# Two narrow fp32 matmuls in place of eighteen in the matmul stream of a two-block transformer kernel

## The reference, cut to what matters

```python
hn = _rmsnorm(x, norm_mix[0]);  x = x + _moba(hn, w_qkv, w_o)          # attention, 16 heads
x = x + _conv_ffn(_rmsnorm(x, norm_ffn[0]), w_up, conv_w, conv_b, w_down)
x = _rmsnorm(x, norm_final)
# second block, with shift, scale and gate vectors from c @ w_mod + b_mod
h = modulate(rms_norm(x, g_ffn1), sh1, sc1)
x = x + 0.5 * (1 + ga1) * swiglu(h, w1_gate, w1_up, w1_down)
h = modulate(rms_norm(x, g_mix), sh2, sc2)
x = x + (1 + ga2) * hybrid_mixer(h, w_in, b_f, g_q, g_k, w_o)          # attention, 8 + 8 heads
h = modulate(rms_norm(x, g_ffn2), sh3, sc3)
x = x + 0.5 * (1 + ga3) * swiglu(h, w2_gate, w2_up, w2_down)
```

## Time and profile before

| | us |
|---|---|
| median of 3 timed executions | 839.67 |
| lowest and highest of them | 838.92, 843.66 |
| the profiled execution, its own time | 841.07 |
| its span, first to last instruction | 838.8 |
| TensorE with a matmul in flight | 811.3 |
| VectorE busy | 645.8 |
| ScalarE busy | 489.4 |

### The profile page before, as it was taken

How to read it: one execution, slowest core, us unless ns; L and a number is a source line. 1 busy time by engine, 2 the same in 40 slices (tenths; PEclk the granted TensorE clock), 3 DMA queues, 4 the chain that set the end, 5 groups by cost and what they waited for, 6 DMA issues and landing times. The chain is left out here.

```text
span 838.8 us, 16840 instructions
## 1 busy us (share of the span) xinstructions
PE 811.3 (97%) x6824; PEld 789.4 (94%) x6824; DVE 645.8 (77%) x1331; ACT 489.4 (58%) x1015; POOL 21.0 (3%) x53
## 2 busy tenths in 40 slices
PE   5999998999999999999999999899998999999998
PEld 5999997999999999999999999789888999999998
DVE  5788878988898796999887777876667896775551
ACT  6755556777666666655554645655655675555440
POOL 1000000000000000000000000700000000000000
PEclk9999999999999999999999999999999999999999
DMA  8776674766665986599988886446334587655540
GB/s 283 256 238 222 213 226 143 226 193 196 225 212 197 318 279 205 183 316 356 318 285 307 276 269 195 108 143 195 111 116 128 175 260 250 200 183 186 188 151 26
DMA packets 150014, 179.44 MB, mean 214 GB/s; under 512 B 5681, under 2 KB 139569, under 8 KB 149937
## 3 DMA queue, kind: packets, MB, share of 16 engines
q1 hardware_dynamic: 148624, 178.17, 65.0%
q0 software_dynamic: 1024, 0.03, 0.1%
q10 hardware_dynamic: 288, 0.16, 0.1%
HBM read 177.27 MB, written 1.05 MB: 213 GB/s over the span
## 5 line engine op out<-in xcount | busy, mean ns | idle before, releaser
L926 DVE TENSOR_TENSOR wlo<-raw,whi 128x512 fp32r<-128x512 f32 x528 | 343.9, 685 | 72.0 <-ACT whi L683 71.3
L1300 PE MATMUL bank<-A,whi 128*128 128x256 f32 x1280 | 366.7, 287 | 12.3 <-DVE wlo L926 7.8
L683 ACT ACTIVATE whi<-raw 128x512 fp32r<-128x512 f32 x528 | 309.0, 622 | 108.1 <-PE bank L1302 104.0
L1301 PE MATMUL bank<-A,whi 128*128 128x256 f32 x1280 | 359.2, 281 | 0.0
L1302 PE MATMUL bank<-A,wlo 128*128 128x256 f32 x1280 | 358.9, 280 | 0.0
L1300 PEld LDWEIGHTS bank<-A,whi 128*128 128x128 f32 x1280 | 245.0, 191 | 15.8 <-DVE wlo L926 9.6
L1301 PEld LDWEIGHTS bank<-A,whi 128*128 128x128 f32 x1280 | 243.2, 190 | 1.0 <-issue 1.0
L1302 PEld LDWEIGHTS bank<-A,wlo 128*128 128x128 f32 x1280 | 242.9, 190 | 0.0
L1300 PE MATMUL bank<-Hhi,whi 128*128 128x256 f32 x528 | 148.0, 280 | 0.0
L1301 PE MATMUL bank<-Hlo,whi 128*128 128x256 f32 x528 | 147.7, 280 | 0.0
L1302 PE MATMUL bank<-Hhi,wlo 128*128 128x256 f32 x528 | 147.7, 280 | 0.0
(11 more groups left out here) (148 smaller groups left out, 784.8 us busy)
## 6 DMA issues: line engine op xcount, KB each, us to landing
mring<-in_w_mod SPq DMA_DIRECT2D x72, 512.0 KB, 6.1
raw<-in_ffn_w_up SPq DMA_DIRECT2D x22, 1024.0 KB, 5.1
raw<-in_w_gate SPq DMA_DIRECT2D x22, 1024.0 KB, 5.5
raw<-in_w_up SPq DMA_DIRECT2D x22, 1024.0 KB, 5.6
raw<-in_w_down SPq DMA_DIRECT2D x16, 1024.0 KB, 5.2
raw<-in_w_in SPq DMA_DIRECT2D x12, 1024.0 KB, 5.7
raw<-in_moba_w_qkv SPq DMA_DIRECT2D x11, 1024.0 KB, 5.7
raw<-in_ffn_w_down SPq DMA_DIRECT2D x8, 1024.0 KB, 6.1
```

What stands on the lines that cost most here:

```text
L683: act.activation(whi[:, i % SPL, k0:k1, 0:width], raw[:, i % RAW, k0:k1, 0:width], ACT.Copy).then_inc(s_whi, 1)
L926: dve.tensor_tensor(lo, raw[:, i % RAW, k0:k1, 0:width], hi.bitcast(F32), ALU.subtract).then_inc(s_wlo, 1)
L1300: pe.matmul(o, hi, xh, start=kg == 0 and not (j and halved(g)), stop=False)
L1301: pe.matmul(o, hi, xl, start=False, stop=False)
```

## The change

The condition of the narrow matmul is replaced. It is no longer issued at slabs 4, 8, 12, 16 and 20 of up1, up2 and up4 and at the first slab of down1, down2 and down4 (18 times), but only at slab 4 of up2 and slab 4 of up4 (2 times), which are the first slabs after the four raw groups. These two were also issued before. The other 16 are gone. Nothing else is changed.

```diff
                 slab = i - plan.first_of[ph]
-                if kt == 0 and (tag == "down" and slab == 0 or ph[:2] == "up" and slab and slab % 4 == 0):
+                if kt == 0 and ph in ("up2", "up4") and slab == RAW_GROUPS[ph]:
                     pe.matmul(banks[NORM_BANK][:, 511:512], meanf[:, :], meanf[:, 0:1], start=True, stop=True)
```

## The result

| | before | after |
|---|---|---|
| median of 20 timed executions | 841.49 us | 838.36 us |
| lowest to highest | 838.25 to 844.33 us | 829.43 to 846.99 us |
| ratio, 95% interval | | 0.994 (0.9922 to 0.9958) |
| the profiled execution, its span | 841.07, 838.8 us | 838.87, 836.6 us |

This ratio and those of the experiments leave out executions more than 1.5% above the lowest of their kernel, here three of the new one's, whose granted clocks (0.991 to 0.994) are those of the others; the medians of all 20 give 0.996. The forecast was 825.7 us, with a range up to 832.4. So the gain is 3 us and not 14, and the new kernel's times spread over 17.6 us where the old one's spread over 6.1 us. That spread is the first sign of what happened.

A forecast was written before the change was run, and what follows sets the result against it. TensorE bounds the kernel: number of matmuls times their pace, plus a few waits. Savings of 3.5, 5.2 and 5.2 us (3.8 own time, 10.1 pace) make 13.9, so 839.67 - 13.9 = 825.7 us, range 824 to 832.4.

The forecast's parts named there:

- The two paces, 113.4 and 117.8 ns, and the switching: Up and down phases: matmuls run fast or slow, 4.4 ns apart; each narrow matmul met in a running stream switches the pace.
- the forecast's 136.0: up2 from slab 8, and down2: 1200 matmuls at the fast pace take 136.0 us, before 141.2, saving 5.2 us.
- Without a foreign matmul in between the pace never changed: Up and down phases: only foreign matmuls change the pace, which held even through the 528 matmuls of a down phase.
- Two of the prediction's own signs of being wrong: Profile after: a phase at 117.8 ns start to end; a pace change inside a phase where no foreign matmul stands.
- the forecast's 157.8: up1 from slab 4, and down1: 1392 matmuls at the fast pace take 157.8 us, before 161.3, saving 3.5 us.
- That the other engines keep up: Fast stretches show no wait; VectorE falls behind by up to 0.7 us in up2 slabs 8 to 11, nothing taken.
- One of the two kept matmuls leaves the slow pace: Rival, up2 or up4: 1392 matmuls cost 4.4 ns more each, 6.1 us, giving 831.8 us; 15%.
- two slow stretches and about no change: Rival: up1 with down1 (1584) and one other stretch (1392) slow, just short of the 3160 for slower; 5%.
- Half clock: Waits ahead of up1 and in qkv3 move with the phase before: zero, bounded by one more short stretch of half clock.

The follow-up runs named there:

- experiment 9: Changed kernel, its two fp32 matmuls replaced by narrow bf16 ones one slab behind the waits, VectorE's second up1 step moved to down1: 829.49 us, 0.9856.
- Experiments 6: Changed kernel, its two fp32 matmuls replaced by five narrow bf16 ones directly behind waits, VectorE's second up1 step moved to down1: 835.08 us, 0.9902.
- experiment 1: The changed kernel again, no edit: 839.43 us, ratio 0.9956 to the kernel before; its profiled execution took 844.58 us.
- Experiment 4: Changed kernel with the three matmuls of a k-tile ordered hi by hi, lo by hi, hi by lo: 840.45 us, 0.9987.
- experiment 11: Changed kernel, its two fp32 matmuls replaced by pairs of narrow fp32 ones at five places one slab behind the waits: 849.82 us, 1.0094.
- experiment 5: Changed kernel, its two narrow fp32 matmuls replaced by five narrow bf16 ones directly behind known waits: 837.13 us, 0.995.

## Why the prediction was wrong

- **The two paces, 113.4 and 117.8 ns, and the switching**: right, and the size of each term with them. Where the new kernel held the fast pace it did what the sum said: 1200 matmuls from slab 8 of up2 to the end of down2 took 504.05 - 368.04 = 136.0 us, the forecast's 136.0. The lowest of the new kernel's 20 times, 829.43 us, is where nearly nothing is slow, as far as can be told without a profile of that execution; experiment 9 holds 829.5. That is 3.8 us above the forecast, but 1.8 of them are the base: the forecast stood on a median of three executions, 839.67 us, and the 20 give 841.49. Against the kernel before in its own group experiment 9 gains 12.1 us of the 13.9 forecast.
- **The step that failed**: "Without a foreign matmul in between the pace never changed", and from it that each phase would keep the pace with which it began. The rule was read from stretches without a wait and from two with one, slab 5 of up2 (0.49 us from start to start) and of up4 (1.08 us), behind which the pace was fast as ahead of them: by luck, as the other profiles show. A wait of about 1 us or less can change the pace as well, and behind it the new kernel has nothing that would change it again. Two of the prediction's own signs of being wrong came so: phases slow from start to end (down1, down4), and changes of pace inside a phase where no foreign matmul stands. I had left these waits out because they cost little: the one at slab 5 of up4 shows in the earlier trace rows as 19.70 us busy in 20.50. In the profile after, the pace and waits so lost took 4.3 us in up1 and down1 (162.1 us for the forecast's 157.8: 720 slow matmuls by 4.4 ns are 3.2, the two waits with their first steps 1.1) and 5.3 us in up4 and down4 (141.3 for 136.0), and 0.6 us more in slabs 5 to 7 of up4.
- **That the other engines keep up**: failed in up1. My reading is that VectorE made up there, while the matmuls went at 117.8 ns, what it fell behind while they went at 113.3. With slabs 4 to 17 all fast in the profile after, the two waits at slabs 14 and 18 appear, 1.1 us. I had looked for this only in up2, where it did not come. Experiments 6 and 9, with the step moved, show none at slab 18.
- **"One of the two kept matmuls leaves the slow pace", 831.8 us at 15%**: still 6.6 us under the measured median. Nearest to it is "two slow stretches and about no change", which had 5%: the profile after has 720 + 1344 slow matmuls in the feed-forward phases, 9.1 us at 4.4 ns. But it came through another mechanism. Both kept ones left the fast pace in the profile after; in that of experiment 1 the one of up2 left the slow one. The chances of slow stretches were much too low, since three or four waits (one or two in up1, one each in up2 and up4) draw in each of the two profiles of the new kernel.
- **Half clock**, "bounded by one more short stretch": the profile after has 3.4 us more of it (granted clock 0.50) at the start of up1, behind the wait of 3.2 us, and 3.4 us at the end of o3, where the last slab takes 7.1 us instead of 5.7. Together some 2.2 us (0.8 and 1.4), so the bound was exceeded in this execution. The new stretch in o3 stood behind a wait of 3.0 us that was there before as well. Six of the 14 profiles have that stretch in o3 and eight have not, all with a wait of 3.0 to 3.1 us there. What decides between them is open.
- **The pace of the old kernel**: it too has waits that may draw, but switches every four slabs, so that about half of each up phase was slow whatever was drawn. That fits its times, which spread over 6.1 us and not 17.6, and a median that holding the drawn pace lowers by only 3 us.
- **The issue gap of the Trainium skill**: "TensorE: Matmul & The Clock Gate", section "Back-to-back issue gap", gives N/2.4 + 2.5 ns for an isolated matmul at full clock, an estimate of 109.2 ns for 256 columns. For a stream of weight loads and matmuls the section says that both set the spacing. This kernel's stream is of the second kind, and neither of its paces, 113.3 and 117.8 ns, is 109.2.

The account of the profiled execution: 13.9 us forecast, less 4.3, 5.3, 0.6 and 2.2, leaves 1.5 us; the span became 2.2 us shorter. The other 0.7 us is that up1 began that much earlier, at 133.85 instead of 134.54; I did not follow that further back.

What stays open: what in TensorE makes the two paces, and what decides behind a wait. Experiment 4 rules out the order of the last two of the three matmuls, and up2 at one DMA share, fast in the profile after and slow in that of experiment 1, speaks against the transfers. Whether the exact moment at which the wait ends decides was not tried.

## What to carry to other kernels

Before an instruction is removed as useless or kept as useful, measure the pace of the stream on both sides of it, and of every wait, from start to start: a state that is set there can be worth more than the instruction. Where a stream has two states and waits draw between them, look at the spread of the times as well as at one profile, and put what sets the good state behind the last wait, not ahead of it and not directly at it. A version that alternates hides the draw in its average; one that holds the state shows it.

## What the runs showed of the hardware

A stream of matmuls of 256 columns, each with its weight load, ran at 113.3 or at 117.8 ns a matmul, at full clock, for up to 1344 matmuls in a row, on the same code. A narrow bf16 matmul of 128 by 128 by 1, at 0.13 us, put it into the faster one each time (31 of 31) where the stream was running; directly behind a wait it left either pace. In the slow pace one weight load of each three lasts longer in the records, in down1 of experiment 11 (slow):
```profile
L1303 PEld LDWEIGHTS bank<-Hhi,wlo 128*128 128x128 f32 x142 | 27.3, 192 | 0.0
L1302 PEld LDWEIGHTS bank<-Hlo,whi 128*128 128x128 f32 x142 | 26.7, 188 | 0.0
```
and in that of experiment 5 (fast) all three have 188 ns, two of them shown:
```profile
L1302 PEld LDWEIGHTS bank<-Hhi,wlo 128*128 128x128 f32 x147 | 27.6, 188 | 0.0
L1300 PEld LDWEIGHTS bank<-Hhi,whi 128*128 128x128 f32 x147 | 27.6, 188 | 0.0
```
It is so in all 42 down phases of the 14 profiles: one load of three at 192 ns in each of the 21 slow ones (the first of a k-tile's three in 8, the second in 6, the third in 7), none in the 21 fast ones. It differs between stretches of the same code, as in down2 (455 to 500 us) and down4 (785 to 825 us) of experiment 1:
```profile
L1302 PEld LDWEIGHTS bank<-Hhi,wlo 128*128 128x128 f32 x128 | 24.6, 192 | 0.0
...
L1301 PEld LDWEIGHTS bank<-Hlo,whi 128*128 128x128 f32 x114 | 21.9, 192 | 0.0
```
So the slow pace has three forms in the records. That fits a pace that depends on how loads and matmuls interlock, but is no proof of it.
